# Last pair of experts in a two-layer diffusion step: the second up units loaded in halves, and their product run by rows

## What is computed

```
def _moe(h, w_router, b_router, w_gate, w_up, w_down):
    ...
    hid = jax.nn.silu(jnp.einsum('nd,edf->enf', n, w_gate)) * jnp.einsum('nd,edf->enf', n, w_up)
    hid = hid * gates.T[:, :, None].astype(hid.dtype)
    return jnp.einsum('enf,efd->nd', hid, w_down).reshape(b, s, d)
```

## Time and profile before

| what | us |
|---|---|
| median of three runs | 1306.06 |
| the profiled execution, its own time | 1306.34 |
| its span, first to last instruction | 1304.4 |
| TensorE busy in the span | 1187.3 (91%) |
| VectorE busy | 279.6 (21%) |
| ScalarE busy | 187.5 (14%) |
| mean granted clock of TensorE | 0.969 of full speed |
| bytes moved | 491.54 MB, mean 377 GB/s |

### The profile page before, as it was taken

How to read it: one execution, slowest core, us unless ns; L and a number is a source line. 1 busy time by engine, 2 the same in 40 slices (tenths; PEclk the granted TensorE clock), 3 DMA queues, 4 the chain that set the end, 5 groups by cost and what they waited for, 6 DMA issues and landing times.

```text
span 1304.4 us, 13903 instructions
## 1 busy us (share of the span) xinstructions
PE 1187.3 (91%) x5455; PEld 514.1 (39%) x5455; DVE 279.6 (21%) x672; ACT 187.5 (14%) x433; POOL 49.7 (4%) x57
## 2 busy tenths in 40 slices
PE   4999989998898989999889999899989899889988
PEld 1455454343333334343344554543424334343422
DVE  1156441101010201101322433311010101101013
ACT  1134321000000001000021342210000001000000
POOL 2212000000000000000011100000000000000000
PEclk8999999999999999999989999899999999999999
DMA  9958988999999999999991578689999999999996
GB/s 366 330 191 343 419 344 364 382 432 426 428 431 428 428 430 429 427 428 430 412 365 58 217 275 338 258 347 385 429 429 428 429 428 428 430 429 428 429 427 251
DMA packets 53610, 491.54 MB, mean 377 GB/s; under 512 B 4642, under 2 KB 5810, under 8 KB 22340
## 3 DMA queue, kind: packets, MB, share of 16 engines
q1 hardware_dynamic: 51376, 485.91, 89.7%
q0 software_dynamic: 2016, 4.94, 1.3%
q10 hardware_dynamic: 180, 0.17, 0.0%
HBM read 488.26 MB, written 2.75 MB: 376 GB/s over the span
## 4 chain that ended last, share of the span: by engine, by line
PE 65%; DMA 22%; issue 6%; SPq 3%; DVE 2%; ACT 1%; POOL 1%; DVEq 0%; ACTq 0%; POOLq 0%
PE bank L884 38%; PE bank L676 10%; DMA ring<-in_w_up 10%; DMA ring<-in_w_gate 9%; PE bank L694 3%; PE bank L853 3%; PE bank L862 2%; PE bank L652 2%; DMA ring<-in_w_in_ab 2%; PE bank L633 1%; DMA ring<-in_w_down 1%; SPq L522 1%; PE bank L905 1%; PE bank L926 1%; SPq L524 1%
## 5 line engine op out<-in xcount | busy, mean ns | idle before, releaser
L884 PE MATMUL bank<-ring,hT 128*64 128x512 f32 x2944 | 672.9, 613 | 77.5 <-issue 38.3
L884 PEld LDWEIGHTS bank<-ring,hT 128*64 128x64 f32 x2944 | 225.2, 141 | 500.2 <-issue 498.1
L676 PE MATMUL bank<-ring,hT 128*128 128x512 f32 (+1 forms) x352 | 151.1, 588 | 5.9 <-DVE hT L1289 3.9
L676 PEld LDWEIGHTS bank<-ring,hT 128*128 128x128 f32 x352 | 67.6, 195 | 82.6 <-issue 76.8
L1561 DVE TENSOR_TENSOR work<-work,bank 128x512 f32<-128x512 f32 x56 | 38.5, 688 | 199.6 <-PE bank L862 199.6
L1554 DVE TENSOR_TENSOR work<-work,bank 128x512 f32<-128x512 f32 x32 | 22.0, 688 | 248.4 <-PE bank L884 248.4
L853 PE MATMUL bank<-work 128*128 128x128 f32 x512 | 59.9, 275 | 0.8 <-DVE work L1534 0.8
L853 PEld LDWEIGHTS bank<-work 128*128 128x128 f32 x512 | 58.8, 192 | 2.5 <-DVE work L1534 2.2
L1165 ACT ACTIVATE hT<-bank 128x512 f32<-128x512 f32 x32 | 19.0, 595 | 282.0 <-PE bank L926 282.0
L1597 DVE COPY work<-bank 128x512 f32<-128x512 f32 x16 | 11.1, 692 | 221.0 <-PE bank L884 204.1
L694 PE MATMUL bank<-ring,work 128*128 128x512 f32 x128 | 56.3, 594 | 0.0
(11 more groups left out here) (176 smaller groups left out, 640.3 us busy)
## 6 DMA issues: line engine op xcount, KB each, us to landing
ring<-in_w_gate SPq DMA_DIRECT2D x64, 2048.0 KB, 17.1
ring<-in_w_up SPq DMA_DIRECT2D x60, 2048.0 KB, 17.2
ring<-in_w_down SPq DMA_DIRECT2D x60, 2048.0 KB, 16.9
ring<-in_w_mod SPq DMA_DIRECT2D x23, 2048.0 KB, 12.3
ring<-in_w_in_c SPq DMA_DIRECT2D x6, 2048.0 KB, 20.4
ring<-in_w_in_ab SPq DMA_DIRECT2D x4, 2048.0 KB, 23.7
work<-in_w_up SPq DMA_DIRECT2D x4, 2048.0 KB, 15.5
ring<-in_w_down SPq DMA_DIRECT2D x8, 1024.0 KB, 17.9
```

What stands on the lines that cost most here:

```text
L676: ins = pe.matmul(b[:, 0:n], hT[:, c, t * P:(t + 1) * P], w[:, c, 0:n], start=c == 0, stop=c == DC - 1)
L884: ins = pe.matmul(bank[banks[j]][64 * e:64 * e + 64, :], lhs[:, 4 * h + c, 64 * e:64 * e + 64], w[e][:, c, j * UC:(j + 1) * UC], start=(h, ...
```

## The change

Units 6 and 7 of the last pair of each layer are now issued like units 10 and 11: as four DMAs of 1 MB, first chunks 0 and 1 of both experts, then chunks 2 and 3 of both. Two semaphores per layer are added for them. `last_product` becomes `product_by_rows` with the unit, the banks and the semaphores as arguments, and the last pair calls it for product 6 as well. The amount of data and the number of matmuls stay as they are.

```diff
-        last_ld = [[sem(f"last_loaded{l}_{h}") for h in range(2)] for l in range(LAYERS)]
+        last_ld = [[sem(f"last_loaded{l}_{h}") for h in range(4)] for l in range(LAYERS)]
...
                     at = [(2 * (PAIRS - 1) + e) * D * D for e in range(2)]
-                    for k in range(MOE_UNITS - 2):
+                    for k in range(MOE_UNITS):
+                        if k in (6, 7, 10, 11):
+                            continue
                         load_in_turn(k, at[k % 2], n * MOE_UNITS + (k + 1))
+                        if k == 5:
+                            in_halves(n, 6, at, a["w_up"], "(p h r) -> h p r")
+                    in_halves(n, 10, at, a["w_down"], "(h p r) -> h p r")
+
+                def in_halves(n, k, at, w, order):
+
                     for half in range(2):
                         for e in range(2):
-                            k = MOE_UNITS - 2 + e
-                            slot = (MOE_AT[l] - AHEAD + k) % SLOTS
-                            src = a["w_down"][l].rearrange("e k n -> (e k n)")[at[e]:at[e] + D * D].rearrange("(h p r) -> h p r", h=2, p=P)[1]
+                            slot = (MOE_AT[l] - AHEAD + k + e) % SLOTS
+                            src = w[l].rearrange("e k n -> (e k n)")[at[e]:at[e] + D * D].rearrange(order, h=2, p=P)[1]
                             if half == 0:
-                                sp.wait_ge(moe_used[l], n * MOE_UNITS + (k + 1))
+                                sp.wait_ge(moe_used[l], n * MOE_UNITS + (k + e + 1))
                             cols = slice(2 * D * half, 2 * D * (half + 1))
-                            sp.dma_start(flat[slot][:, cols], src[:, cols]).then_inc(last_ld[l][half], 16)
+                            sp.dma_start(flat[slot][:, cols], src[:, cols]).then_inc(last_ld[l][(k - 6) // 2 + half], 16)
...
-                def last_product(n):
+                def product_by_rows(n, k, banks, lhs, ready, half_done):
-
-                    k = MOE_UNITS - 2
                     slots = [(MOE_AT[l] - AHEAD + k + e) % SLOTS for e in range(2)]
-                    pe.wait_ge(m["ht_ready"], 2 * n + 2)
+                    pe.wait_ge(ready, 2 * n + 2)
                     for half in range(2):
-                        pe.wait_ge(last_ld[l][half], 32)
+                        pe.wait_ge(last_ld[l][(k - 6) // 2 + half], 32)
...
                             if (half, j) == (1, 0):
-                                ins.then_inc(m["down_half"], 1)
+                                ins.then_inc(half_done, 1)
...
-                    product(n, 6, (2, 3), hgT, m["hg_ready"], m["up_half"])
+                    if final:
+                        product_by_rows(n, 6, (2, 3), hgT, m["hg_ready"], m["up_half"])
+                    else:
+                        product(n, 6, (2, 3), hgT, m["hg_ready"], m["up_half"])
```

More of the change, by code:

```diff
@@ L904, in last_product @@
                                 for e in range(2):
-                                    ins = pe.matmul(bank[6 + j][64 * e:64 * e + 64, :], hidT[:, 4 + c, 64 * e:64 * e + 64],
+                                    ins = pe.matmul(bank[banks[j]][64 * e:64 * e + 64, :], lhs[:, 4 + c, 64 * e:64 * e + 64],
                                                     rows4[slots[e]][:, c, j * UC:(j + 1) * UC],
@@ L957, in pair @@
                     if final:
-                        last_product(n)
+                        product_by_rows(n, 10, (6, 7), hidT, m["ht_ready"], m["down_half"])
                     else:
```

## The result

The changed kernel takes 1311.01 us (median of six runs, 1309.82 to 1313.46), against 1306.76 us before (six runs, 1306.03 to 1307.72). The ratio is 1.0032, with a 95% interval of 1.0019 to 1.0045: slower by 4.2 us. The profiled execution of the changed kernel took 1311.48 us, with a span of 1309.5 us; its granted clock is 0.967 on average. One run of a later set of nine of the changed kernel took 1523.85 us at a mean granted clock of 0.75, against 0.964 to 0.970 in the other eight, for a reason that no run here shows; it stands in no ratio.

The account below looks back on a forecast made before the run. The prediction took the stream of weights as the bound. Layer 0 (0 + 0.1 + 1.7 = +1.8 us) and layer 1 (-0.5 + 0.1 + 1.7 = +1.3) added 3.1 to 1306.34, giving 1309.4 us; range 1306.0 to 1311.2.

Parts of the forecast that it names:

- the second rival: Clock stays down longer: 2.8 us lost on one or both products 8 of the last pairs, 1310.5 to 1311.6 us; chance 0.12.
- the sum: Whole kernel: +1.8 us in layer 0 and +1.3 in layer 1, together +3.1 on 1306.34, so 1309.4 us.
- What bounds: Whole kernel: the weights' stream bounds it, two units every 9.8 to 9.9 us; TensorE needs 7.09 us for each 9.8.
- Product 6: Last pair, both layers: starts right after product 4, ending 4.3 us earlier in layer 1 and 2.6 in layer 0.
- The idle time moves in front of product 8: Last pair, both layers: TensorE's gap between transposes and product 8 becomes 3.7 to 3.8 us, ended by unit 9's landing.
- What is won: Start of product 8 in the last pair: 0.5 us earlier in layer 1, nothing won in layer 0.
- The DMAs: Last pair: two more issues per layer cost nothing; loading in halves puts 0.1 us on unit 9's landing in each layer.
- The rival that the halves flow worse: Unit 9 lands 1.0 us later in each layer, on top of slow products 8: 1311.2 us; chance 0.04.
- The clock: Product 8 of both last pairs runs slow behind the longer gap, costing 1.69 us each.
- The first rival: Clock holds at product 8 in one layer or both: 1307.7 us with one slow product, 1306.0 with none; chance 0.30.
- The clock's rule: Product 8, both layers: by the skill's rule alone the clock's fall would be certain; by the profile's rows it is likely.
- The base: Starting time of the forecast: the profiled execution's 1306.34 us, 0.28 us above the median of 1306.06.

## Why the prediction was right, and where its size was off

Slower, by an amount beyond 0.2%, was the likeliest case (0.54), and the measured 1311.0 us lies in the range of 1306.0 to 1311.2, near its top. The mechanism is the one forecast; the size is not. The result is nearer to the lower value of the second rival (1310.5, chance 0.12) than to the 1309.4 of the sum, and the profile is what that rival described: one product slow for 2.92 us and one for 1.69. Its sign, a product of over 9 us, is there in layer 0. The number is in the range only because the top of the range was taken from that rival. Step by step:

*What bounds.* That the weights' stream is the bound and product 8 starts with unit 9's landing: right. In layer 1 unit 9 lands at 1264.69 + 20.17 = 1284.86, and product 8 starts at 1284.95, by the chain of the changed kernel:

```profile
1264.69 20.17 DMA ring<-in_w_down
1284.86 0.09 issue
1284.95 8.78 PE bank L891 x32
```

*Product 6.* Right: it starts at once and takes 7.1 us in both layers. The wait for `up_half` is hidden as said: VectorE is done with the first half at 1277.72 + 0.69 = 1278.4, before the transposes start at 1279.26.

*The idle time moves in front of product 8.* Right in kind; it measured 4.1 us where the sum had 3.7.

*What is won.* Layer 0 nothing, as said. Layer 1: 0.31 us, where the sum had 0.5 - 0.1 = 0.4.

*The DMAs.* Two more issues cost nothing. Unit 9 is at most 0.06 us later in layer 0, and in layer 1 it lands 19.7 us after unit 5 (which landed at 1243.5 + 21.6 = 1265.1), for 19.6 before: the guess was 0.1. While the new halves are under way, the changed kernel moves 424 GB/s (615 to 625 us); before moved 426 GB/s in the same work (614 to 624 us). The Trainium skill's figure for a load of 1 MB, 341 GB/s, from "DMA: Bandwidth & Descriptors", section Bandwidth, is not what a full queue of such loads shows here. The rival that the halves flow worse is refuted by the kernel that loads halves and waits for whole units (1.0003).

*The clock.* This is the term of the sum that was mis-sized. I took 1.7 us for each slow product 8. Six such products behind a gap of 4.1 us were recorded, in the changed kernel twice and in the kernels with one layer changed; they took 10.01, 8.78, 9.78, 9.08, 8.77 and 9.63 us. Their mean is 9.34 us, which is 2.25 us over 7.09. With that the sum is 2 x 2.25 - 0.31 + 0.06 = 4.3 us, against 4.2 measured. The rows that I priced it by stood behind gaps of at most 2.9 us; the 2.8 us of the earlier trace rows, which I had kept for a rival, came true in part of the cases. In the four products of over 9 us the granted clock was 0.50 for at least the last 0.7 us before the product; in the two of 8.8 us it was 1.00 until the product began. One of each kind, from the windows just before product 8, with layer 1 changed alone and then with layer 0 changed alone:

```profile
1284.60:1285.30 0.70, 0.00 (x0) 0.02 (x1) 0.67 (x2) 0.00 (x0) 0.00 (x0) 0.50 1.04 433
...
633.00:634.00 1.00, 0.01 (x2) 0.04 (x2) 0.96 (x3) 0.00 (x0) 0.00 (x0) 1.00 0.96 401
```

So the second rival holds half of the truth: a longer gap makes not only a fall more likely, but also a longer stay. All ten profiled executions together bear this out. Of the products of an expert pair (7.09 us at full clock) that stand behind an idle time, none of 134 was slow behind up to 1.7 us, 26 of 74 behind 1.7 to 2.5 us, 59 of 105 behind 2.5 to 2.7 us, 52 of 60 behind 2.8 to 3.0 us, and all six behind 4.1 us. Of the 137 slow ones behind the shorter gaps one took over 9 us, of the six behind 4.1 us four did. The one is outside the changed places, in layer 1 of the changed kernel:

```profile
1187.00 10.07 PE L891 MATMUL bank<-ring,hT 128*64 128x512 f32 x32 [2.84 <-DMA ring<-in_w_gate]
```

That the fall itself was close to certain was right: six of six. The first rival, a clock that holds, came true only where the gap was filled.

*The clock's rule.* The Trainium skill, "TensorE: Matmul & The Clock Gate", section Why this matters for your kernels, advises against idle gaps between bursts of matmuls. The traces agree: six of six products 8 behind 4.1 us were slow, one of two behind 2.4 us, and none behind the 0.7 and 0.8 us that the filler left.

*The base.* With more runs the median of before rose from 1306.06 to 1306.76 and 1307.03 us. The 1309.4 us of the forecast were built on an execution of 1306.34, so 0.4 us of the distance of 1.6 us to the result are that base; the clock's term, 2 x (2.25 - 1.69) = 1.1 us, is nearly all the rest.

Still open is how often product 8 is slow for 1.7 us and how often for nearly 3: six records are too few.

## What to carry to other kernels

Where a stream of loads at full rate sets the time, starting one product earlier moves idle time to the next wait and wins next to nothing by itself (0.3 us here); ask where the idle time goes. Here time was won only when every load up to the last was split, which left less to do after the last landing. Whether the halves of units 8 and 9 alone would have done it, with units 6 and 7 whole, was not run. Two short idle times can be cheap where their sum in one place is not: a gap of 2.5 us often slowed the product behind it, but most of that went into the slack that followed, while a gap of 4.1 us cost TensorE's clock each time, and the product behind it 2.25 us on average with no slack left. Filling such a gap with useless matmuls brought the time back, and is a quick test of whether the clock is the cause.

## What the runs showed that I had not expected

How long the clock stays down: product 8 lost 2.9, 2.7 and 2.5 us in three of six records and 1.7 to 2.0 us in the other three. And how little the size of a load matters in a full queue: eight loads of 0.5 MB in a row still moved 411 GB/s, next to 421 to 428 GB/s for loads of 1 and 2 MB, and the last bytes of the layer landed 0.6 us later for it.
